# Bias tables of eight heads by one product and one spreading transfer, in a hybrid mLSTM, sparse-attention and mixture-of-experts layer

## The chip, the cores and the metric

The kernel runs on one core of a Trainium2 chip. The metric is the device time of one execution in microseconds (us), lower is better. The core has five engines that run their own instruction streams and meet at semaphores: TensorE (PE, matrix products), VectorE (DVE), ScalarE (ACT), GpSimd (POOL) and SyncE (SP, which here only issues transfers). ACT also issues transfers, from its own queue.

## The reference

One layer over 528 tokens (16 meta tokens and 512 real ones) of width 1024. After a layer norm, one wide projection feeds two branches: an mLSTM branch, and an attention branch that picks the 128 best keys of each query by an index score. Their outputs are gated, projected and normed, and a mixture of 16 experts follows. The part that matters here is the bias that the attention adds to its logits, a table lookup by bucket of the distance between query and key:

```python
def _rel_bucket(dist):
    n = jnp.maximum(dist, 0)
    nf = jnp.maximum(n, REL_MAX_EXACT).astype(jnp.float32)
    large = REL_MAX_EXACT + (jnp.log(nf / REL_MAX_EXACT) / math.log(REL_MAX_DIST / REL_MAX_EXACT)
                             * (REL_BUCKETS - REL_MAX_EXACT)).astype(jnp.int32)
    large = jnp.minimum(large, REL_BUCKETS - 1)
    return jnp.where(n < REL_MAX_EXACT, n, large)

        l_sel = jnp.einsum('bqhr,bqkr->bqhk', ql, c_sel) + \
            rel_bias[_rel_bucket(t[None, :, None] - sel)].transpose(0, 1, 3, 2)
        l_sel = jnp.where(valid[:, :, None, :], l_sel.astype(jnp.float32), -jnp.inf)
        p = jax.nn.softmax(jnp.concatenate([l_meta.astype(jnp.float32), l_sel], axis=-1), axis=-1)
```

`rel_bias` has 32 buckets by 8 heads. The bias depends only on the distance, so for one head it is one row of 656 numbers, and each query reads that row with its own shift.

## The kernel before

Every engine's program is one straight list in the code, and that order is the order of its work. Nothing is moved by a scheduler.

**The tables.** A one-hot matrix `oneh` (32 buckets by 656 distances) and `rel_bias` in `relb` (32 by 8) are loaded first. For each head h, `tables` on PE (L1057 to L1064) takes column h of `relb`, repeated 128 times, as the 32 by 128 weights and `oneh` as the moving operand, in two matmuls of 512 and 144 columns. That gives the head's row 128 times over, one copy in each of the 128 partitions of the accumulator `wide[h % 2]`. ACT copies it to one of four buffers in `ftab` (`tables_out`, L662) and issues a transfer of 328 KB to `table_dram[h]` (`tables_store`, L668). Eight such transfers write 8 x 128 equal rows to memory. Much later SP loads `strips` (L429) with a stride of 655 elements between rows of 656, which shifts each partition by one place: that is the bias of each query.

**Where they stand on PE.** Two heads at a time, between the projections:

- `tables(0)` at the very start, before the transposes of the input (L1075);
- `tables(2)` after the first unit's product, whose accumulators end with `kv_done`, and before `by_channel` of block `B_QI`;
- `tables(4)` after block `B_QI + 1`, and behind it the four small transposes L1126, which wait for `c_ready`;
- `tables(6)` after those transposes and before `channel_unit(2, B_QA)`.

**The projections around them.** The weights of the input projection come in units of 1 MB. SP loads a unit into `raw` (L394), ACT makes the high part `w_hi` (`split_hi`, L654), DVE the low part `w_lo` (`split_lo`, L1481), and PE multiplies three times (L1027, L1028, L1029: high by high, and the two mixed products). One 128 by 512 block is 24 such matmuls.

**The step that `c_ready` stands for.** PE transposes the compressed keys (L1116 to L1121, `ckv_done`), ACT squares them (L716), ACT does `split_hi(2)`, DVE does `split_lo(2)`, and DVE writes `c_tok` (L1530, `c_ready`). Before the squares ACT has three small functions on `rows` (L706 to L708), which in the kernel before stand behind `tables_out(2)`. DVE then goes on with scans on `rows` (L1535 to L1542), `widx`, which needs L1126, and `split_lo(3)`. The rounds of top-k on DVE start when ACT has put out the first index scores (L748), which PE makes in `index_scores(0)` (L1111) after `channel_unit(2, B_QA)`.

**Memory on the chip.** `ftab` lies where `v_ext` lies later. For that reason POOL waits at L550 for all eight stores before it writes the ones of `v_ext` (L552).

Of the kernel before, what the change touches and what calls it, by code (L numbers as in the profile page):

```python
# [8 lines left out]
F32 = mybir.dt.float32  # L9
# [6 lines left out]
ACT = mybir.ActivationFunctionType  # L16
# [3 lines left out]
P = 128  # L20
# [9 lines left out]
AH, AD = 8, 64  # L30
# [3 lines left out]
BUCKETS, MAX_EXACT, MAX_DIST = 32, 16, 128  # L34
# [22 lines left out]
FX = STRIP + P - 1 + 1  # L57
# [27 lines left out]
def build(nc, a, onehot, router_const, entries, no_token, slot_numbers, out, h_dram, table_dram, h1_dram, list_dram, y_dram):  # L85
    w_in = a["w_in"][0].rearrange("(c p) n -> p c n", p=P)
    with ExitStack() as ctx:
        base = 16640

        def at(name, shape, dtype, kb):  # L90
            return nc.alloc_sbuf_tensor_at(name, shape, dtype, offset=base + int(kb * 1024))

        def sem(name):
            return ctx.enter_context(nc.semaphore(name))
# [7 lines left out]
        def little(name, shape, dtype=F32):  # L102
# [40 lines left out]
        relb = little("relb", [BUCKETS, AH])  # L143
# [18 lines left out]
        A0 = 62.0  # L162
# [43 lines left out]
        ftab = at("ftab", [P, 4, FX], F32, A0 + 51)  # L206
        oneh = at("oneh", [BUCKETS, FX], F32, A0 + 139.5)
# [47 lines left out]
        wide = [ctx.enter_context(nc.psum_tensor(f"wide{i}", [P, 1024], F32)) for i in range(2)]  # L255
# [9 lines left out]
            table_in wuk_loaded table_done table_out strips_loaded  # L265
# [14 lines left out]
            late_consts z_added var1_ready rstd1_ready h1t_done h1t_used h1t_out h1_ready h1_stored gained  # L280
# [6 lines left out]
        q = {n: sem(n) for n in names}  # L287
        x_loaded = [sem(f"x_loaded{i}") for i in range(TT + 1)]
        table_stored = [sem(f"table_stored{i}") for i in range(2)]
# [91 lines left out]
        def _(sp):  # L381
# [42 lines left out]
            for stored in table_stored:  # L424
                sp.wait_ge(stored, 16 * AH // 2)
# [70 lines left out]
        def _(pool):  # L496
# [53 lines left out]
            for stored in table_stored:  # L550
                pool.wait_ge(stored, 16 * AH // 2)
# [95 lines left out]
        def _(act):  # L647
# [8 lines left out]
            def tables_out(h0):  # L656

                for h in (h0, h0 + 1):
                    act.wait_ge(q["table_done"], h + 1)
                    if h >= 4:  # L660
                        act.wait_ge(table_stored[h % 2], 16 * (h // 2))
                    nc.scalar.activation(ftab[:, h % 4, :], wide[h % 2][:, 0:FX], ACT.Copy).then_inc(q["table_out"], 1)  # L662

            def tables_store(h0):

                for h in (h0, h0 + 1):
                    act.wait_ge(q["table_out"], h + 1)
                    act.dma_start(table_dram[h], ftab[:, h % 4, :]).then_inc(table_stored[h % 2], 16)  # L668

            tables_out(0)  # L670

            for i in range(TT):
# [20 lines left out]
            tables_store(0)  # L693
# [9 lines left out]
            tables_out(2)  # L703
            tables_store(2)
# [308 lines left out]
        def _(pe):  # L1013
# [43 lines left out]
            def tables(h0):  # L1057

                for h in (h0, h0 + 1):
                    if h >= 2:  # L1060
                        pe.wait_ge(q["table_out"], h - 1)
                    rb = relb[:, h:h + 1].to_broadcast([BUCKETS, P])
                    nc.tensor.matmul(wide[h % 2][:, 0:512], rb, oneh[:, 0:512], start=True, stop=True)
                    nc.tensor.matmul(wide[h % 2][:, 512:FX], rb, oneh[:, 512:FX], start=True, stop=True).then_inc(q["table_done"], 1)  # L1064


            pe.wait_ge(q["table_in"], 32)
            tables(0)

            pe.wait_ge(q["table_out"], 2)  # L1070
# [44 lines left out]
            tables(2)  # L1115
# [7 lines left out]
            tables(4)  # L1123
# [4 lines left out]
            tables(6)  # L1128
            channel_unit(2, B_QA)
            pe.wait_ge(q["table_out"], AH)  # L1130
# [56 lines left out]
            for h in range(MH + 1):  # L1187
# [808 lines left out]
```

## Time and profile before

| | us |
|---|---|
| median of 3 runs | 871.2 |
| the runs | 869.11, 871.20, 873.55 |
| the profiled execution, device time | 869.1 |
| its span in the trace | 867.0 |
| PE busy | 761.4 (88% of the span) |
| DVE busy | 588.9 (68%) |
| ACT busy | 429.5 (50%) |
| POOL busy | 103.2 (12%) |

The span is the time from the first to the last record of the trace, and 2.1 us of the device time lie around it. "Idle before" is the time that an engine did nothing before an instruction, with the instruction or transfer that released it. The chain of waits is read backwards from the last instruction and shows only what the end waited for. PEclk is the clock that TensorE was granted: 1.00 is 2.4 GHz, 0.50 is 1.2 GHz, and a number between the two is a stretch that had both.

### The profile page before, as it was taken

The page shows a single profiled execution, that of the slowest core. Times are in us where ns is not written, and L with a number is a line of the kernel's source. Part 1 is how long each engine was busy: PE and PEld are TensorE (multiplying, and loading weights), DVE is VectorE, ACT ScalarE, POOL GpSimd, SP SyncE. Part 2 cuts the span into 40 slices and gives each one's busy share as a digit, 9 for nine tenths or more (in the row PEclk, how much of TensorE's full clock was granted, in tenths as well). Part 3 has the DMA queues.
Part 4 walks back from the last instruction along what each step waited for, and adds up shares of the span by engine and source line. Part 5 has one row for each costly group of instructions (what it writes and reads, how often), then busy time and mean ns, then how long its engine had stood idle before and what let it go on. Part 6 is the DMA issues. An engine that isn't in the chain of part 4 may idle for free.

```text
span 867.0 us, 10824 instructions
## 1 busy us (share of the span) xinstructions
PE 761.4 (88%) x3991; PEld 612.9 (71%) x3991; DVE 588.9 (68%) x794; ACT 429.5 (50%) x497; POOL 103.2 (12%) x118
## 2 busy tenths in 40 slices
PE   4499999999898787999999874899999999999920
PEld 2387799897566446887888773788888888888720
DVE  4905899795346644222464868788989888889838
ACT  5344433434542655322122130678787787787713
POOL 4630000000001000000000111212121111112012
PEclk9999999999999898999999975999999999999975
DMA  7744121310070300135126974699999999996143
GB/s 192 228 153 160 49 87 61 98 49 1 0 246 1 98 1 1 49 98 194 50 96 221 408 262 137 224 334 409 403 395 393 400 398 394 392 388 264 62 174 138
DMA packets 102644, 167.07 MB, mean 193 GB/s; under 512 B 18960, under 2 KB 39696, under 8 KB 102608
## 3 DMA queue, kind: packets, MB, share of 16 engines
q1 hardware_dynamic: 95024, 145.53, 47.4%
q0 software_dynamic: 4752, 13.11, 3.9%
q10 hardware_dynamic: 2832, 7.93, 2.3%
q8 instruction: 24, 0.39, 0.2%
q14 instruction: 12, 0.10, 0.0%
HBM read 153.38 MB, written 17.40 MB: 197 GB/s over the span
## 4 chain that ended last, share of the span: by engine, by line
PE 79%; DVE 8%; ACT 5%; issue 3%; DMA 2%; SPq 1%; POOL 0%; POOLq 0%; DVEq 0%; ACTq 0%
PE low L1027 15%; PE low L1028 15%; PE low L1029 15%; PE wide L1027 7%; PE wide L1029 7%; PE wide L1028 7%; PE wide L1390 2%; ACT prob L860 2%; PE low L1211 1%; PE low L1274 1%; PE low L1342 1%; PE wide L1196 1%; SPq L394 1%; PE low L1208 1%; PE low L1397 1%
## 5 line engine op out<-in xcount | busy, mean ns | idle before, releaser
L1760 DVE TENSOR_TENSOR m_lo<-m_raw,m_hi 128x2048 fp32r<-128x2048 f32 x95 | 215.0, 2290 | 30.2 <-ACT m_hi L906 29.6
L906 ACT ACTIVATE m_hi<-m_raw 128x2048 fp32r<-128x2048 f32 x95 | 179.7, 1917 | 27.8 <-PE low L1029 27.8
L1481 DVE TENSOR_TENSOR w_lo<-raw,w_hi 128x2048 fp32r<-128x2048 f32 x28 | 64.1, 2290 | 81.0 <-ACT w_hi L654 80.6
L1027 PE MATMUL low<-m_hi,xe_hi 128*128 128x512 f32 x256 | 104.4, 408 | 3.6 <-DVE xe_lo L1825 3.2
L1027 PE MATMUL low<-hT_hi,w_hi 128*128 128x512 f32 (+1 forms) x240 | 94.0, 392 | 10.6 <-issue 10.6
L1028 PE MATMUL low<-m_lo,xe_hi 128*128 128x512 f32 x256 | 101.5, 397 | 0.0
L1029 PE MATMUL low<-m_hi,xe_lo 128*128 128x512 f32 x256 | 101.4, 396 | 0.0
L1028 PE MATMUL low<-hT_lo,w_hi 128*128 128x512 f32 (+1 forms) x240 | 93.3, 389 | 0.0
L1029 PE MATMUL low<-hT_hi,w_lo 128*128 128x512 f32 (+1 forms) x240 | 92.6, 386 | 0.0
L654 ACT ACTIVATE w_hi<-raw 128x2048 fp32r<-128x2048 f32 x28 | 53.5, 1909 | 17.8 <-PE wide L1029 8.3
L1027 PEld LDWEIGHTS low<-hT_hi,w_hi 128*128 128x128 f32 x240 | 46.9, 195 | 20.9 <-issue 11.1
L1027 PEld LDWEIGHTS low<-m_hi,xe_hi 128*128 128x128 f32 x256 | 49.0, 191 | 17.2 <-DVE m_lo L1760 4.0
L1029 PEld LDWEIGHTS low<-m_hi,xe_lo 128*128 128x128 f32 x256 | 49.0, 192 | 10.9
L1028 PEld LDWEIGHTS low<-m_lo,xe_hi 128*128 128x128 f32 x256 | 49.0, 192 | 9.3
L1029 PEld LDWEIGHTS low<-hT_hi,w_lo 128*128 128x128 f32 x240 | 46.9, 195 | 9.1
L1028 PEld LDWEIGHTS low<-hT_lo,w_hi 128*128 128x128 f32 x240 | 46.8, 195 | 9.1 <-issue 0.2
L1027 PE MATMUL wide<-m_hi,hd_hi 128*128 128x512 f32 x128 | 51.3, 401 | 1.6 <-DVE hd_lo L1834 1.6
L1029 PE MATMUL wide<-m_hi,hd_lo 128*128 128x512 f32 x128 | 50.1, 391 | 0.0
L1028 PE MATMUL wide<-m_lo,hd_hi 128*128 128x512 f32 x128 | 49.8, 389 | 0.0
L730 ACT ACTIVATE gate<-low 128x512 f32<-128x512 f32 x16 | 9.6, 598 | 61.8 <-PE low L1029 61.8
L938 ACT ACTIVATE xe_hi<-wide 128x1024 fp32r<-128x1024 f32 x16 | 16.4, 1026 | 43.8 <-PE wide L1390 43.8
L1027 PE MATMUL wide<-hT_hi,w_hi 128*128 128x264 f32 x128 | 36.9, 288 | 1.1 <-ACT relu L748 1.0
(341 smaller groups left out, 1479.5 us busy)
## 6 DMA issues: line engine op xcount, KB each, us to landing
m_raw<-in_w_gate SPq DMA_DIRECT2D x32, 1024.0 KB, 9.4
m_raw<-in_w_up SPq DMA_DIRECT2D x32, 1024.0 KB, 8.7
m_raw<-in_w_down SPq DMA_DIRECT2D x31, 1024.0 KB, 10.4
raw<-in_w_in SPq DMA_DIRECT2D x19, 1024.0 KB, 5.5
raw<-in_w_out SPq DMA_DIRECT2D x4, 1024.0 KB, 4.9
table_dram<-ftab ACTq DMA_DIRECT2D x8, 328.0 KB, 3.2
strips<-table_dram SPq DMA_DIRECT2D x8, 264.0 KB, 4.2
xn<-in_x SPq DMA_DIRECT2D x4, 512.0 KB, 5.6
```

The costliest lines, as they stand in the source:

```text
L394: sp.dma_start(unit3(raw, u % RAW, u)[:, :, to:to + n], src).then_inc(raw_loaded[u % RAW], 16)
L654: nc.scalar.activation(w_hi[:, u % SPL, :], raw[:, u % RAW, :], ACT.Copy).then_inc(q["hi_ready"], 1)
L730: nc.scalar.activation(dst, src, func).then_inc(q["block_out"], 1)
L860: nc.scalar.activation(prob[:, h, 0:w], prob[:, h, 0:w], ACT.Exp, scale=-1.0, bias=nmax[:, h:h + 1], accum_out=psums[:, h:h + 1]).then_inc ...
L906: nc.scalar.activation(m_hi[n % MS][:, :], (m_spare if is_last(n, j) else m_raw[slot])[:, :], ACT.Copy).then_inc(q["m_hi_ready"], 1)
L938: nc.scalar.activation(xe_hi[:, :, :], wide[1][:, :].rearrange("p (c x) -> p c x", c=KC), ACT.Copy).then_inc(q["xe_hi_ready"], 1)
L1027: nc.tensor.matmul(outp, lh, rh, start=first, stop=False)
L1028: nc.tensor.matmul(outp, lh, rl, start=False, stop=False)
L1029: return nc.tensor.matmul(outp, ll, rh, start=False, stop=last)
L1390: mm = nc.tensor.transpose(wide[1][:, c * P:(c + 1) * P], xg[slot][:, c * P:(c + 1) * P], ident[:, :])
L1481: v.tensor_tensor(w_lo[:, u % SPL, :], raw[:, u % RAW, :], w_hi[:, u % SPL, :].bitcast(F32), ALU.subtract).then_inc(q["lo_ready"], 1)
L1760: v.tensor_tensor(m_lo[n % MS][:, :], (m_spare if is_last(n, j) else m_raw[n % MR])[:, :], m_hi[n % MS][:, :].bitcast(F32), ALU.subtract). ...
```

## The change

PE makes one pair of matmuls with the whole of `relb` (32 by 8) as weights: 8 output rows, one for each head. ACT copies them once to `ftab`, now 8 partitions by 656 at another address, and stores them to a new tensor in memory, `table_row`, 8 by 656. After `split_hi(3)`, ACT waits for that store and issues one transfer from memory to memory whose source names each row 128 times. It writes the same `table_dram` as before. The other three `tables` calls on PE, the copies and stores that went with them on ACT, and the waits on them are gone, on POOL too.

```diff
-        ftab = at("ftab", [P, 4, FX], F32, A0 + 51)
+        ftab = at("ftab", [AH, FX], F32, A0 + 128)
...
             sp.wait_ge(q["st_done"], MH)
-            for stored in table_stored:
-                sp.wait_ge(stored, 16 * AH // 2)
+            sp.wait_ge(q["table_stored"], 16)
...
             step(nc.gpsimd.memset(pre[:, :, 0:CONV - 1], 0.0))
-            for stored in table_stored:
-                pool.wait_ge(stored, 16 * AH // 2)
...
-            tables_out(0)
+            act.wait_ge(q["table_done"], 1)
+            nc.scalar.activation(ftab[:, :], wide[0][0:AH, 0:FX], ACT.Copy).then_inc(q["table_out"], 1)
+            act.wait_ge(q["table_out"], 1)
+            act.dma_start(table_row, ftab[:, :]).then_inc(q["table_put"], 16)
...
             split_hi(1)
-            tables_store(0)
...
             act.wait_ge(q["load_late"], 16 * 10)
-            tables_out(2)
-            tables_store(2)
...
             evac(B_QI, qidxT[:, 0, :])
-            tables_out(4)
-            tables_store(4)
             evac(B_QI + 1, qidxT[:, 1, :])
             split_hi(3)
-            tables_out(6)
-            tables_store(6)
+            act.wait_ge(q["table_put"], 16)
+            act.dma_start(table_dram, table_row.rearrange("h (o f) -> h o f", o=1).to_broadcast([AH, P, FX])).then_inc(q["table_stored"], 16)
...
             pe.wait_ge(q["table_in"], 32)
-            tables(0)
-
-            pe.wait_ge(q["table_out"], 2)
+            nc.tensor.matmul(wide[0][0:AH, 0:512], relb[:, :], oneh[:, 0:512], start=True, stop=True)
+            nc.tensor.matmul(wide[0][0:AH, 512:FX], relb[:, :], oneh[:, 512:FX], start=True, stop=True).then_inc(q["table_done"], 1)
+            pe.wait_ge(q["table_out"], 1)
...
-            tables(2)
             by_channel(take(B_QI)[:, :], 1, 0, META, T).then_inc(q["block_done"], 1)
...
             by_channel(take(B_QI + 1)[:, :], 1, P, META, T).then_inc(q["block_done"], 1)
-            tables(4)
             pe.wait_ge(q["c_ready"], TT + 1)
...
             mm.then_inc(q["wt_done"], 1)
-            tables(6)
             channel_unit(2, B_QA)
-            pe.wait_ge(q["table_out"], AH)
             pe.wait_ge(q["block_out"], B_QI + 2)
```

Line numbers of the changed kernel differ from here on: L1007, L1008 and L1009 are the products L1027, L1028 and L1029, and L1094 is the transpose L1126.

On PE, the place between block `B_QI + 1` (its last matmuls stand first) and `channel_unit(2, B_QA)`, before the change:

```order
171 L1028 MATMUL low<-hT_lo,w_hi 128x512
172 L1029 MATMUL low<-hT_hi,w_lo 128x512
173 L1063 MATMUL wide<-oneh,relb 128x512 [waits table_out]
174 L1064 MATMUL wide<-oneh,relb 128x144
175 L1063 MATMUL wide<-oneh,relb 128x512 [waits table_out]
176 L1064 MATMUL wide<-oneh,relb 128x144
177 L1126 MATMUL low<-ident,smallT 128x8 [waits c_ready]
178 L1126 MATMUL low<-ident,smallT 128x8 x3
179 L1063 MATMUL wide<-oneh,relb 128x512 [waits table_out]
180 L1064 MATMUL wide<-oneh,relb 128x144
181 L1063 MATMUL wide<-oneh,relb 128x512 [waits table_out]
182 L1064 MATMUL wide<-oneh,relb 128x144
```

The same place on PE after the change:

```order
165 L1008 MATMUL low<-hT_lo,w_hi 128x512
166 L1009 MATMUL low<-hT_hi,w_lo 128x512
167 L1094 MATMUL low<-ident,smallT 128x8 [waits c_ready]
168 L1094 MATMUL low<-ident,smallT 128x8 x3
169 L1007 MATMUL low<-hT_hi,w_hi 128x512 [waits lo_ready,hi_ready,block_out]
```

The transposes that wait for `c_ready` now follow the block directly, and the next projection follows them.

On ACT, the place from `split_hi(2)` (a `w_hi` row) to the copies of `qaT`, before the change:

```order
34 L654 ACTIVATE w_hi<-raw 128x2048 [waits kv_done,raw_loaded2]
35 L730 ACTIVATE qidxT<-low 128x512 [waits block_done,h_stored]
36 L662 ACTIVATE ftab<-wide 128x656 [waits table_stored0,table_done]
37 L662 ACTIVATE ftab<-wide 128x656 [waits table_stored1,table_done]
38 L668 DMA table_dram<-ftab 128x656 [waits table_out] x2
39 L730 ACTIVATE qidxT<-low 128x512 [waits block_done]
40 L654 ACTIVATE w_hi<-raw 128x2048 [waits block_done,raw_loaded0]
41 L662 ACTIVATE ftab<-wide 128x656 [waits table_stored0,table_done]
42 L662 ACTIVATE ftab<-wide 128x656 [waits table_stored1,table_done]
43 L668 DMA table_dram<-ftab 128x656 [waits table_out] x2
44 L730 ACTIVATE qaT<-low 128x512 [waits block_done] x2
```

The same place on ACT after the change:

```order
31 L650 ACTIVATE w_hi<-raw 128x2048 [waits kv_done,raw_loaded2]
32 L712 ACTIVATE qidxT<-low 128x512 [waits block_done,h_stored]
33 L712 ACTIVATE qidxT<-low 128x512 [waits block_done]
34 L650 ACTIVATE w_hi<-raw 128x2048 [waits block_done,raw_loaded0]
35 L719 DMA table_dram<-table_row 1024x1x656 [waits table_put]
36 L712 ACTIVATE qaT<-low 128x512 [waits block_done] x2
```

Four copies and four stores have left this stretch, and one transfer with its wait has come behind `split_hi(3)`.

## Rows read from the trace of the kernel before

**Rows 1.** The page, the chain of waits by engine, shares of the span.

```profile
PE 79%; DVE 8%; ACT 5%; issue 3%; DMA 2%; SPq 1%; POOL 0%; POOLq 0%; DVEq 0%; ACTq 0%
```

**Rows 2.** The chain of waits in order of time: start, length, engine, tile, line.

```profile
54.47 1.05 PE wide L1063 x2
...
56.87 0.43 PE low L1027
57.30 0.23 PE low L1028
...
68.77 1.05 PE wide L1063 x2
...
71.19 0.84 PE wide L1063 x2
...
73.38 0.72 PE low L1027
74.10 0.43 PE low L1028
...
76.97 0.23 PE low L1029
```

**Rows 3.** Timeline of PE from 68 us: start, length, engine, line, tiles.

```profile
70.78 0.29 PE L1126 MATMUL low<-ident,smallT 8*128 8x8 f32 x2
...
71.01 1.02 PE L1063 MATMUL wide<-oneh,relb 32*128 32x512 f32 x2
```

**Rows 4.** Timelines of ACT and DVE from 36 us, idle time in brackets.

```profile
58.03 0.73 ACT L706 ACTIVATE rows<-smallT,bif 4x528 f32<-4x528 f32 x1 [0.41 <-ACT ftab L662]
...
63.23 0.28 ACT L716 ACTIVATE md<-low 128x128 f32<-128x128 f32 x1 [1.84 <-PE low L1120]
...
67.15 2.29 DVE L1481 TENSOR_TENSOR w_lo<-raw,w_hi 128x2048 fp32r<-128x2048 f32 x1 [1.46 <-ACT w_hi L654]
69.36 1.37 DVE L1530 SCALAR_TENSOR_TENSOR c_tok<-low,crs,kvg 128x128 f32<-128x128 f32 x5
...
76.79 2.29 DVE L1481 TENSOR_TENSOR w_lo<-raw,w_hi 128x2048 fp32r<-128x2048 f32 x1
87.80 0.35 DVE L1556 TENSOR_SCALAR score<-relu,widx 128x256 f32<-128x256 f32 x1 [8.71 <-ACT relu L748]
```

**Rows 5.** Stretches: busy time and count of each engine, PEclk, DMA share, GB/s.

```profile
69.80:73.20 3.40, 3.40 (x19) 1.90 (x17) 3.30 (x7) 2.31 (x4) 0.00 (x0) 1.00 0.79 234
73.20:76.60 3.40, 3.40 (x10) 2.62 (x9) 3.23 (x6) 2.20 (x2) 0.00 (x0) 0.52 0.77 275
```

**Rows 6.** PE's timeline at three later gaps, and the stretches of 3 us behind them.

```profile
219.18 1.16 PE L1192 MATMUL low<-rows,sel_row 4*128 4x512 f32 x2 [2.55 <-DVE dw L1646]
...
219.00:222.00 3.00, 2.83 (x4) 0.42 (x4) 0.72 (x2) 1.80 (x3) 0.00 (x0) 0.68 0.00 0
...
317.02 0.40 PE L1247 MATMUL wide<-khT,qaT 64*128 64x16 f32 x4 [2.28 <-DVE nmax L1683]
...
318.00:321.00 3.00, 2.66 (x20) 1.71 (x20) 1.68 (x5) 1.41 (x4) 0.00 (x0) 1.00 0.00 0
...
327.85 0.40 PE L1247 MATMUL wide<-khT,qaT 64*128 64x16 f32 x4 [2.66 <-DVE nmax L1683]
...
330.00:333.00 3.00, 3.00 (x17) 2.57 (x15) 1.34 (x5) 1.39 (x3) 0.00 (x0) 0.55 0.00 0
```

**Rows 7.** Transfers: table stores, the strips' issues, SP's loads of units.

```profile
table_dram<-ftab ACTq DMA_DIRECT2D x8, 328.0 KB, 3.2
...
L429 SPq DMA_DIRECT2D strips<-table_dram x8: 339/432/547, 243.3 to 246.5; - x8
...
69.47 31.16 SPq L394 DMA_DIRECT2D raw<-in_w_in  x3
```

**Rows 8.** Timeline of ACT in the first 10 us.

```profile
8.12 0.72 ACT L662 ACTIVATE ftab<-wide 128x656 f32<-128x656 f32 x1 [1.47 <-PE wide L1064]
...
9.23 1.24 ACT L674 ACTIVATE xn<-xn,shift,rstd 128x1024 f32<-128x1024 f32 x1 [0.39 <-DVE shift L1488]
```

More of the change, by code:

```diff
@@ L82, in bcast_rows, with build @@
     return bass.AP(tensor=ap.tensor, offset=ap.offset + offset, ap=[[0, P], [1, n]])
-def build(nc, a, onehot, router_const, entries, no_token, slot_numbers, out, h_dram, table_dram, h1_dram, list_dram, y_dram):
+def build(nc, a, onehot, router_const, entries, no_token, slot_numbers, out, h_dram, table_row, table_dram, h1_dram, list_dram, y_dram):
     w_in = a["w_in"][0].rearrange("(c p) n -> p c n", p=P)
@@ L264, in build @@
             const_done vec_step act_step pool_step zero_done
-            table_in wuk_loaded table_done table_out strips_loaded
+            table_in wuk_loaded table_done table_out table_put table_stored strips_loaded
             load_consts load_late
@@ L279, in build @@
             z_part h_loaded  vm_ready
-            late_consts z_added var1_ready rstd1_ready h1t_done h1t_used h1t_out h1_ready h1_stored gained
+            late_consts z_added var1_ready rstd1_ready h1t_done h1t_used h1t_out h1_ready h1_stored
             router_done scores_ready chosen_ready  dest_ready  listed lists_loaded lists_ready
@@ L288, in build @@
         x_loaded = [sem(f"x_loaded{i}") for i in range(TT + 1)]
-        table_stored = [sem(f"table_stored{i}") for i in range(2)]
         gathered = [sem(f"gathered{i}") for i in range(2)]
@@ L654, in split_hi @@
                 nc.scalar.activation(w_hi[:, u % SPL, :], raw[:, u % RAW, :], ACT.Copy).then_inc(q["hi_ready"], 1)
[L656 to L668, printed above, removed]
-            tables_out(0)
+            act.wait_ge(q["table_done"], 1)
+            nc.scalar.activation(ftab[:, :], wide[0][0:AH, 0:FX], ACT.Copy).then_inc(q["table_out"], 1)
+            act.wait_ge(q["table_out"], 1)
+            act.dma_start(table_row, ftab[:, :]).then_inc(q["table_put"], 16)
             for i in range(TT):
@@ L1055, in by_token @@
                 return mm
[L1057 to L1064, printed above, removed]
             pe.wait_ge(q["table_in"], 32)
-            tables(0)
-            pe.wait_ge(q["table_out"], 2)
+            nc.tensor.matmul(wide[0][0:AH, 0:512], relb[:, :], oneh[:, 0:512], start=True, stop=True)
+            nc.tensor.matmul(wide[0][0:AH, 512:FX], relb[:, :], oneh[:, 512:FX], start=True, stop=True).then_inc(q["table_done"], 1)
+            pe.wait_ge(q["table_out"], 1)
             pe.wait_ge(q["const_done"], 1)
@@ L1982 @@
     h_dram = nc.dram_tensor("h_dram", (S, D), F32, kind="Internal").ap()
+    table_row = nc.dram_tensor("table_row", (AH, FX), F32, kind="Internal").ap()
     table_dram = nc.dram_tensor("table_dram", (AH, P, FX), F32, kind="Internal").ap()
@@ L1993 @@
     y_dram = nc.dram_tensor("y_dram", (2 * S, D), F32, kind="Internal").ap()
-    build(nc, a, oh, router_const, entries, no_token, slot_numbers, out, h_dram, table_dram, h1_dram, list_dram, y_dram)
+    build(nc, a, oh, router_const, entries, no_token, slot_numbers, out, h_dram, table_row, table_dram, h1_dram, list_dram, y_dram)
     return run(nc, [arrays], core_ids=[0]).results[0]["out"]
```

## The prediction

> **What bounds the kernel now.** I read the chain of waits first, because the change takes work off PE and that is worth something only where PE is what the end waits for. 79% of the span hangs on PE [rows 1]. In the order of time the chain runs through the three later table calls. From 54.47 to 56.87 us it is the tables of heads 2 and 3, from 68.77 to about 70.8 those of heads 4 and 5, from 71.19 to 73.38 those of heads 6 and 7, each with PE products right before and right behind [rows 2]. The first table call, at 3 to 8 us, is not in the chain at all. Next I read the timelines of PE, DVE and ACT around 70 us, to see what would be late once the tables are gone [rows 3, 4]. Then I read the granted clock there and behind other gaps of PE [rows 5, 6], and last the transfers [rows 7].
>
> **The start.** Two heads' tables, two copies and two buffers become one pair of matmuls, one copy and one small store. ACT's second copy ran from 8.12 to 8.84 us, and ACT then stood idle 0.39 us until DVE's shift released it for the first tile of the input at 9.23 [rows 8]. So DVE was the later one there, and the copy that goes gives back nothing. The new store is issued by ACT behind the first copy, about 6.7 us. A table store costs ACT's queue some 0.4 us, which fits before 9.23. Worth: 0.
>
> **Tables of heads 2 and 3.** They hold PE, in the chain, from 54.47 to 56.87: 2.40 us [rows 2]. The block behind them needs nothing of ACT that is late: it uses unit 1, split long before. It starts 2.40 us earlier, and so do the transposes of the compressed keys behind it. Worth: 2.40.
>
> **Tables of heads 4 and 5.** Here the gain goes. Before the change PE ends these tables at about 70.8 and starts the small transposes L1126 at 70.78 [rows 3]. Those wait for `c_ready`, and DVE ended `c_tok` at 69.36 + 1.37 = 70.73 [rows 4]. Table work and wait end together, so the tables were filling a wait of PE. How far does `c_ready` move? Follow it back. DVE's `c_tok` stands right behind `split_lo(2)` at 67.15, which ACT's `w_hi` released. That follows ACT's squares, the first of which, at 63.23, had been idle 1.84 us for PE's transposes [rows 4]. So the whole row of steps hangs on PE and moves by the same 2.40 us. ACT's three functions on `rows` ran before the squares and started at 58.03, behind a table copy [rows 4]. They move at least as far, since the copies ahead of them go. So `c_ready` comes at 70.73 - 2.40 = 68.33. Block `B_QI + 1` ends at 68.77 - 2.40 = 66.37 [rows 2]. PE now stands idle from 66.4 to about 68.4, where it computed tables before. The call was 2.0 us long and the new wait is 2.0 us long. Worth: 0.
>
> **Tables of heads 6 and 7.** They stand behind the transposes, from 71.19 to 73.38 in the chain: 2.19 us [rows 2]. `channel_unit(2)` needs the split of unit 2, which DVE ends before `c_tok`. Worth: 2.19. Its start moves from 73.38 to 68.79, that is 2.40 + 2.19 = 4.59 us. The PE timeline gives nearly the same (the transposes start at 70.78 and the tables 0.23 later [rows 3], so 4.6 to 4.7).
>
> **Does it pass through?** DVE ends the scans and starts `split_lo(3)` at 76.79, and then idles 8.71 us until ACT's first index scores, at 87.80 [rows 4]. Those come from PE, behind `channel_unit(2)`. DVE's own work ahead of the idle moves by 2.4 us and has 8.71 us of slack, less the 2.2 us by which PE moves further. So DVE, too, starts its top-k rounds 4.6 us earlier. ACT loses four copies of 0.72 us there, as the one shown [rows 8], and gets one issue. POOL's write to `v_ext` moves earlier and nobody waits for it yet. SP's unit loads wait for DVE's `lo_ready`, and move with it. Every later stage starts on one of these.
>
> **The clock.** Through the stretch in which PE ran tables of 32 rows, 69.8 to 73.2, the granted clock was 1.00, and in the next, 73.2 to 76.6, it was 0.52 [rows 5], so nearly all at 1.2 GHz. The 8 matmuls from 73.38 to 76.97 took 3.59 us [rows 2]. At the 0.23 us of the full clock they take 1.87, plus 0.20 for the first of a block (0.43 at 56.87 against 0.23 behind it). So the fall cost 1.5 us. After the change PE idles 2.0 us and then does only tiny transposes for 0.2 to 0.4. Does the clock fall again? Three gaps of PE in this trace are near. Behind 2.55 us of idle the next 3 us had 0.68, behind 2.66 us the stretch from 330 us had 0.55, and behind 2.28 us the clock stayed at 1.00 [rows 6]. With its transposes the new gap is 2.2 to 2.4 us, just among them. At one end the fall stays as it was (worth 0), at the other it goes (worth 1.5). I take 0, since two of three near gaps fell, but it is close to even, and the next run may differ from the last one.
>
> **The transfer.** It writes the same 2.6 MB as the eight stores did. The stores landed after 3.2 us each [rows 7], so 8 in a row take at most 25.6 us. The new one also reads memory, so up to twice that by this estimate, 51 us. It starts behind `split_hi(3)`, at about 69 us (the block before it ends at 66.4, and two short ACT instructions and the split of 1.9 follow), and SP's first load of strips is issued at 243.3 [rows 7], 4.6 us earlier after the change: about 170 us of cover. It shares the engines with the loads of units 6 and 7, issued in the stretch from 69.47 to 100.6 [rows 7]. These are 1 MB each and are split on ACT some 30 us or more behind their issue, so a few us more are hidden. Worth: 0. If the cover were gone it would cost its length beyond 170 us.
> The rows show nothing of how a repeated source is spread over the 16 DMA engines. The Trainium skill, "DMA: Bandwidth & Descriptors", section "Rules for kernel authors", says that the slowest dimension of the access patterns sets the number of engines, so that an outermost dimension under 16 confines a transfer to at most so many. The source here has 8 rows outermost, which would mean 8 engines, a doubling of the 51 us to about 100, an estimate. It would still be under the cover. No row of before shows it.
>
> **Sum.** 0 + 2.40 + 0 + 2.19 + 0 = 4.6 us. The profiled execution took 869.1 (867.0 of span and 2.1 around it), so it becomes 864.5. The median of the runs stands 2.1 above it. From the median, 871.2 - 4.6 = 866.6.
>
> **Rivals.**
> (a) The clock holds. Then 1.5 us more are gained: 6.1, which gives 865.1. For it: the gap at 317 us, and that the tables of 4.6 us in a row, the longer stretch of poor work, are gone. Against it: the other two gaps.
> (b) The clock pays more than before. The fall comes with a second one, since every later gap of PE meets the clock at another moment. One fall costs 1.5, as worked out above: 4.6 - 1.5 = 3.1, which gives 868.1.
> (c) The gain is hidden anyway. If `c_ready` or the first index scores depended on something that doesn't move (a load, a store), PE would wait there up to the old time: gain 0 to 2.4, 871.2 to 868.8. Against it: each step above was released by PE or its followers [rows 4].
> (d) Slower: the transfer is confined to very few DMA engines. If the eight stores at 3.2 us were spread over all 16 and this one is on one, it takes 8 x 3.2 x 16 = 410 us, from 69 to 479, and SP's wait for it ends 240 us late: about 1107. It decides from 170 us on, that is 6.6 times the 25.6. Below that it costs nothing. For it, only the odd shape of the source. Against it: 128 rows for each head.
>
> **How the numbers follow.** Forecast 0.45, (a) 0.30, (b) 0.14, (c) 0.08, (d) 0.03. The range takes in the forecast, (a) and most of (b), and for its ends the medians' own scatter, since three runs of before spread over 4.4 us: 863.2 to 869.8. About 0.5%, 4.4 us, is what a measurement of this kernel can tell from no change, so the line is at 866.8, right beside the forecast. Of the forecast a bit over half falls under it (0.27), of (a) nearly all (0.28), of the rest 0.02: faster 0.57. Slower, (d) and a bad draw of the clock: 0.05. The rest, 0.38, is the same.
>
> **What would show each step.** PE has two table matmuls, at about 3 us, and none later. Block `B_QI` starts at about 54.4. The four transposes wait for DVE's `c_tok` with about 2.0 us idle of PE before them, and start at 68.4. `channel_unit(2)` starts at 68.8. The first score on DVE comes at about 83.2, with idle time before it as now. The clock behind 68.8 tells forecast from (a): 0.5 or 1.00 for some 3 us. The spreading transfer lands before 170 us. The prediction is wrong if PE's wait for `c_ready` is longer than 2.3 us, if the strips' issues move by other than 4 to 6 us, or if the distance between them and the end of the span changes by over 2 us.

## The result, and the profile after

| | before | after |
|---|---|---|
| median, us | 869.45 (6 runs) | 863.5 (6 runs) |
| lowest to highest | 866.82 to 873.55 | 860.06 to 865.65 |
| profiled execution, device time | 869.1 | 863.86 |
| its span | 867.0 | 861.9 |
| PE busy | 761.4 | 751.6 |

The ratio of after to before is 0.9925, 95% interval 0.9903 to 0.9948: 6.5 us less, 4.5 to 8.4 (the two medians differ by 6.0). The kernel is faster by more than the 0.5% that this measurement can tell. The forecast had been 4.6 us, so the way was right and the size, by the best estimate, too small; 4.6 lies just inside the interval. The absolute time, 863.5, lies at the very edge of the range of 863.2 to 869.8. Measured once more beside other kernels, the change came to 0.9939 (0.9919 to 0.9959), 5.3 us.

On the page of after, the end still hangs on PE, as in [rows 1]:

```profile
PE 751.6 (87%) x3961; PEld 605.7 (70%) x3963; DVE 588.9 (68%) x794; ACT 424.6 (49%) x490; POOL 103.5 (12%) x118
...
PE 78%; DVE 8%; ACT 6%; issue 4%; DMA 2%; SPq 1%; POOL 1%; POOLq 0%; DVEq 0%; ACTq 0%
```

The timeline of PE after the change, in place of the tables of [rows 2, 3] (start, length, engine, line, tiles, idle time before in brackets):

```profile
65.00 0.39 PE L1009 MATMUL low<-hT_hi,w_lo 128*128 128x512 f32 x1
67.40 0.41 PE L1094 MATMUL low<-ident,smallT 8*128 8x8 f32 x4 [2.02 <-DVE c_tok L1496]
67.74 0.50 PE L1007 MATMUL low<-hT_hi,w_hi 128*128 128x512 f32 x1
...
69.57 0.63 PE L1007 MATMUL low<-hT_hi,w_hi 128*128 128x512 f32 x1
...
72.43 0.40 PE L1008 MATMUL low<-hT_lo,w_hi 128*128 128x512 f32 x1
```

The block ends at 65.2, PE stands idle for 2.02 us, released by DVE's `c_tok`, and the next projection starts at 67.74, where it was at 73.3. The first four matmuls behind it still start 0.23 to 0.34 us apart; from 68.8 to about 72.2 they start 0.43 apart.

ACT and DVE around it, answering [rows 4]:

```profile
59.84 0.28 ACT L698 ACTIVATE md<-low 128x128 f32<-128x128 f32 x1 [2.05 <-PE low L1089]
...
63.77 2.29 DVE L1447 TENSOR_TENSOR w_lo<-raw,w_hi 128x2048 fp32r<-128x2048 f32 x1 [1.46 <-ACT w_hi L650]
65.98 1.36 DVE L1496 SCALAR_TENSOR_TENSOR c_tok<-low,crs,kvg 128x128 f32<-128x128 f32 x5
...
82.25 0.35 DVE L1522 TENSOR_SCALAR score<-relu,widx 128x256 f32<-128x256 f32 x1 [6.54 <-ACT relu L728]
```

The row of steps is the same as before: the squares wait for PE's transposes, the low part of the split for ACT's high part, `c_tok` for the split. The first score on DVE comes 5.55 us earlier than in [rows 4], and DVE still idles ahead of it.

The stretches of 3 us with the granted clock (third number from the right), answering [rows 5]:

```profile
66.00:69.00 3.00, 1.60 (x9) 1.40 (x10) 2.90 (x9) 1.82 (x2) 0.00 (x0) 0.97 0.49 138
69.00:72.00 3.00, 3.00 (x8) 2.32 (x8) 2.91 (x3) 0.00 (x0) 0.00 (x0) 0.50 0.95 314
72.00:75.00 3.00, 3.00 (x14) 2.36 (x13) 2.89 (x4) 0.00 (x0) 0.00 (x0) 0.96 0.52 197
```

The clock fell to 1.2 GHz at about 68.8, 1.1 us into the projection behind the gap. Before the change it fell behind the tables.

ACT's rows at the same place show when the spreading transfer was issued:

```profile
65.52 0.77 ACTq L719 DMA_DIRECT2D table_dram<-table_row  x1
65.92 1.90 ACT L650 ACTIVATE w_hi<-raw 128x2048 fp32r<-128x2048 f32 x1
```

In the code the transfer stands behind `split_hi(3)`, the second row. In the trace it was issued at 65.52, before that split began at 65.92.

The start, answering [rows 8], and the issues of the strips, answering [rows 7]:

```profile
8.71 1.24 ACT L659 ACTIVATE xn<-xn,shift,rstd 128x1024 f32<-128x1024 f32 x1 [2.10 <-DVE shift L1454]
...
L427 SPq DMA_DIRECT2D strips<-table_dram x8: 339/432/609, 237.8 to 241.1; - x8
```

ACT now idles 2.10 us ahead of the first tile, again released by DVE. The strips start at 237.8, 5.5 us earlier than before, and the span is 5.1 us shorter. Not all of the 5.5 is the change: the last product of the first unit, which stands ahead of the tables of heads 2 and 3, already came 0.8 us earlier in this profile (53.42 against 54.19, shown below).

### The profile page after: what moved, and what is told of

Its sections match the earlier page's. It is cut to its first block, busy times and chain, and to the rows that moved or that the text cites. A ratio compares the mean times of both kernels' runs of the same rounds, so it can differ in the third digit from the quotient of the medians.

```text
span 861.9 us, 10746 instructions
## 1 busy us (share of the span) xinstructions
PE 751.6 (87%) x3961; PEld 605.7 (70%) x3963; DVE 588.9 (68%) x794; ACT 424.6 (49%) x490; POOL 103.5 (12%) x118
## 4 chain that ended last, share of the span: by engine, by line
PE 78%; DVE 8%; ACT 6%; issue 4%; DMA 2%; SPq 1%; POOL 1%; POOLq 0%; DVEq 0%; ACTq 0%
PE low L1007 15%; PE low L1009 15%; PE low L1008 15%; PE wide L1007 7%; PE wide L1009 7%; PE wide L1008 7%; PE wide L1356 2%; ACT prob L840 2%; PE low L1177 1%; ACT w_hi L650 1%; PE wide L1162 1%; PE low L1308 1%; PE low L1240 1%; SPq L393 1%; PE low L1174 1%
## 5 line engine op out<-in xcount | busy, mean ns | idle before, releaser
L1007 PE MATMUL low<-m_hi,xe_hi 128*128 128x512 f32 x256 | 103.9, 406 | 3.6 <-DVE xe_lo L1791 3.2
L1007 PE MATMUL low<-hT_hi,w_hi 128*128 128x512 f32 (+1 forms) x240 | 93.6, 390 | 10.6 <-issue 10.6
L1009 PE MATMUL low<-m_hi,xe_lo 128*128 128x512 f32 x256 | 100.8, 394 | 0.0
L1008 PE MATMUL low<-m_lo,xe_hi 128*128 128x512 f32 x256 | 100.4, 392 | 0.0
L1008 PE MATMUL low<-hT_lo,w_hi 128*128 128x512 f32 (+1 forms) x240 | 93.2, 388 | 0.0
L1009 PE MATMUL low<-hT_hi,w_lo 128*128 128x512 f32 (+1 forms) x240 | 92.7, 386 | 0.0
L1007 PEld LDWEIGHTS low<-hT_hi,w_hi 128*128 128x128 f32 x240 | 46.8, 195 | 20.6 <-issue 11.0
L1007 PEld LDWEIGHTS low<-m_hi,xe_hi 128*128 128x128 f32 x256 | 48.6, 190 | 17.2 <-DVE m_lo L1726 4.4
L1009 PEld LDWEIGHTS low<-m_hi,xe_lo 128*128 128x128 f32 x256 | 48.5, 189 | 10.9
L1008 PEld LDWEIGHTS low<-m_lo,xe_hi 128*128 128x128 f32 x256 | 48.7, 190 | 9.2
L1008 PEld LDWEIGHTS low<-hT_lo,w_hi 128*128 128x128 f32 x240 | 46.6, 194 | 9.2 <-issue 0.2
L1009 PEld LDWEIGHTS low<-hT_hi,w_lo 128*128 128x128 f32 x240 | 46.7, 194 | 9.0
L1007 PE MATMUL wide<-m_hi,hd_hi 128*128 128x512 f32 x128 | 51.3, 401 | 1.6 <-DVE hd_lo L1800 1.6
L1009 PE MATMUL wide<-m_hi,hd_lo 128*128 128x512 f32 x128 | 50.1, 392 | 0.0
L1008 PE MATMUL wide<-m_lo,hd_hi 128*128 128x512 f32 x128 | 49.8, 389 | 0.0
L1007 PE MATMUL wide<-hT_hi,w_hi 128*128 128x264 f32 x128 | 36.9, 288 | 1.1 <-ACT relu L728 1.0
```

What stands on the lines that cost most here:

```text
L1007: nc.tensor.matmul(outp, lh, rh, start=first, stop=False)
L1008: nc.tensor.matmul(outp, lh, rl, start=False, stop=False)
L1009: return nc.tensor.matmul(outp, ll, rh, start=False, stop=last)
```

## A measure that doesn't depend on the start

Two profiles of one kernel can differ by a few us, so a comparison of two spans is weak. The first dense product (L1027 of before) started at 39.85, 39.77 and 38.42 us in three profiles of the same kernel before, and the three spans were 867.0, 871.3 and 867.3. I therefore use stretches between two events in one profile: **A**, from PE's transposes of the compressed keys (L1120, L1089 after) to DVE's first score (L1556, L1522), and **B**, from that first score to the first issue of the strips. All 14 profiles, in us:

| kernel | A | B |
|---|---|---|
| before, first profile | 25.2 | 155.5 |
| before, second | 26.8 | 155.6 |
| before, third | 25.2 | 157.2 |
| before, split first | 26.8 | 155.5 |
| no first pair | 26.9 | 155.5 |
| no second pair | 26.8 | 155.5 |
| no third pair | 26.7 | 155.5 |
| no fourth pair | 21.4 | 157.2 |
| change, first profile | 23.0 | 155.6 |
| change, second | 23.0 | 155.6 |
| change, POOL waits | 23.0 | 155.5 |
| change, gap filled | 21.4 | 155.6 |
| change, split first | 19.4 | 155.6 |
| change, split first, other spreading | 19.4 | 155.6 |

B is 155.5 or 155.6 in all but two, so nothing between the first score and the strips depends on the tables. A takes few values, and they are what the experiments below explain.

The tables of heads 2 and 3 stand ahead of A and are not in it. What they held is read between the last product of the first unit and the transposes. Before:

```profile
54.19 0.28 PE L1029 MATMUL low<-hT_hi,w_lo 128*128 128x264 f32 x1
54.40 1.12 PE L1063 MATMUL wide<-oneh,relb 32*128 32x512 f32 x2
...
56.80 0.50 PE L1027 MATMUL low<-hT_hi,w_hi 128*128 128x512 f32 x1
57.14 0.40 PE L1028 MATMUL low<-hT_lo,w_hi 128*128 128x512 f32 x1
...
62.59 0.60 PE L1120 MATMUL low<-ident,cT 128*128 128x128 f32 x4
...
73.31 0.79 PE L1027 MATMUL low<-hT_hi,w_hi 128*128 128x512 f32 x1
```

After:

```profile
53.42 0.28 PE L1009 MATMUL low<-hT_hi,w_lo 128*128 128x264 f32 x1
53.54 0.40 PE L1007 MATMUL low<-hT_hi,w_hi 128*128 128x512 f32 x1
...
59.21 0.60 PE L1089 MATMUL low<-ident,cT 128*128 128x128 f32 x4
```

From the start of the first row to the transposes it is 62.59 - 54.19 = 8.40 us before and 59.21 - 53.42 = 5.79 after. The seven profiles with those tables have 8.40 or 8.41, the seven without them 5.78 or 5.79: the call held PE for 2.6 us.

The stretch behind B, from the first issue of the strips to the end, is where single profiles scatter: 621.8 to 628.3 us over the 14. The six profiles of before in which the tables of heads 4 to 7 are all left have a mean of 625.0 there, and the six of the change and its variants 625.0 as well. So nothing of the gain is seen there, and much of the scatter of the times is.

## The experiments

### One pair of tables at a time

Each of the first four takes one `tables` pair out of the kernel before, with its copies and stores. For the first pair:

```diff
-            tables_out(0)
...
-            tables_store(0)
...
-            tables(0)
-
-            pe.wait_ge(q["table_out"], 2)
```

and the counts of the semaphores go down by two heads. The others are the same for `tables(2)`, `tables(4)` and `tables(6)`.

> The kernel before without the table matmuls, copies and stores of heads 0 and 1 at the start (those two heads' bias is left out; their strips are loaded from heads 2 and 3). Theory of the prediction: DVE releases the first tile of the input, so the start gives nothing: same as before, and the first dense product starts at about 39.8 us as before. Rival: the start is the source of the surplus of the change, 0.7 to 1.5 us faster, and the first dense product starts at about 39.1 us.

Ratio 1.0008 (0.9986 to 1.0031): no difference, 869.0 against 869.4. The interval reaches down to 1.2 us less, so the times alone don't exclude the lower part of the rival's 0.7 to 1.5. The first dense product starts at 39.51, but three profiles of before spread from 38.42 to 39.85, so that number decides nothing. The row of ACT for the first tile of the input decides:

```profile
9.27 1.24 ACT L675 ACTIVATE xn<-xn,shift,rstd 128x1024 f32<-128x1024 f32 x1 [7.18 <-DVE shift L1487]
```

With no table work ahead of it ACT stood idle for 7.18 us and still began at 9.27, where it began at 9.23 in [rows 8]: DVE sets this time, and the start gives nothing.

> The kernel before without the tables of heads 2 and 3 (left out; their strips come from heads 4 and 5). Theory: PE gets back 2.40 us in full, since everything behind follows PE, and the wait for c_ready moves with it: 2.4 us faster. Rival: something that doesn't move holds c_ready or the scores, and the gain is under 1 us.

Ratio 0.9978 (0.9956 to 1.0001), 1.9 us less with an interval from 0 to 3.8. It holds the 2.4 and leans against the rival's "under 1", but doesn't exclude it. The profile is clearer: the next block follows the first unit's product directly, and from that product to the transposes it is 5.79 us in place of 8.40, so 2.6 less. A behind it, 26.8, is a value that before has too. So nothing that doesn't move took the gain back.

> The kernel before without the tables of heads 4 and 5 (left out; their strips come from heads 6 and 7). Theory: they filled PE's wait for c_ready, so PE stands idle 2.0 us in their place and the gain is 0 to 0.2 us. Rival: the copies on ACT that go with them also delayed c_ready or later work, and the gain is 1 to 2 us.

Ratio 0.9996 (0.9977 to 1.0016), 0.3 us: nothing, as the theory had it, though the interval reaches to 2.0 less and so doesn't exclude the rival. The timeline of PE in this kernel does:

```profile
68.68 0.22 PE L1126 MATMUL low<-ident,smallT 8*128 8x8 f32 x1 [2.02 <-DVE c_tok L1530]
```

The wait of 2.02 us stands where the tables were. From the transposes of the compressed keys to these small ones it is 8.20 us, and 8.19 in before and after: the copies that went too did not bring `c_ready` forward. Removing the call gave nothing because it had filled a wait of the same length.

> The kernel before without the tables of heads 6 and 7 (left out; their strips come from heads 0 and 1). Theory: PE gets back 2.19 us. If the clock fell because of 4.6 us of table work in a row, it now sees only 2.1 us of it and may hold: then 3.7 us. Rival: the clock falls as before in most runs and the gain stays at 2.2.

Ratio 0.9966 (0.9949 to 0.9983), 3.0 us less (1.5 to 4.4), between the two, and both are inside the interval. In its profile the clock held where the kernel before fell to 0.72 and 0.50:

```profile
69.00:72.00 3.00, 3.00 (x19) 2.50 (x18) 2.90 (x4) 2.21 (x3) 0.00 (x0) 1.00 0.99 301
72.00:75.00 3.00, 3.00 (x15) 2.44 (x14) 2.83 (x6) 0.91 (x1) 0.00 (x0) 1.00 0.71 262
```

A is 21.4, against 25.2: 3.8 less, that is 2.19 of tables and 1.6 of clock. B, though, is 157.2 here, 1.7 longer: behind the gap of PE that ends at 213.6 us the clock stayed down for longer than it did behind the same gap in the first profile of before. So of the 3.8 only 2.1 are left by the time the strips are issued (A + B is 178.6 against 180.7; against the later profiles of before, with 182.3 and 182.4, it is 3.7). With 2.1 us of table work in a row the clock held at the tables in this one profile, and with 4.6 us it fell in every one.

### The change again, and the clock behind the gap

> The changed kernel itself, timed once more, beside the next three. Theory of the prediction: the steps give 4.6 us, so the ratio to the kernel before is 0.9947, and the larger gain first measured was scatter of the draws. Rival: there is something more in the change, and the ratio stays at 0.9925 (6.5 us).

Ratio 0.9939 (0.9919 to 0.9959), 5.3 us, between the theory's 4.6 and the rival's 6.5, and both are inside the interval. Timing alone can't tell them apart. The profile shows A at 23.0 once more.

The next one fills the gap of PE with work of its own:

```diff
+            for i in range(8):
+                nc.tensor.matmul(bank[4][:, :], hT_hi[:, i, 0:P], hT_hi[:, i, META:T], start=(i == 0), stop=(i == 7))
             pe.wait_ge(q["c_ready"], TT + 1)
```

> The changed kernel with 8 dense matmuls of 128 x 512 (1.9 us, result unused) put into PE's 2.0 us of idle before the transposes that wait for c_ready. Theory: the fall of the clock behind the gap comes from PE standing idle; with dense work in it the clock holds and the kernel is 1.5 us faster than the change. Rival: the fall has to do with something else (its place in time), it stays, and the time is that of the change.

Ratio to before 0.9928 (0.991 to 0.9945), median 863.1 against 864.1 of the change in the same series. The intervals of the two ratios overlap for the most part, so the times don't settle it. The profile does: PE's filler (first row) is followed by stretches at the full clock.

```profile
63.96 2.02 PE L1093 MATMUL wide<-hT_hi 128*128 128x512 f32 x8
...
66.00:69.00 3.00, 2.88 (x15) 2.42 (x16) 2.86 (x5) 0.56 (x1) 0.00 (x0) 1.00 0.85 276
69.00:72.00 3.00, 3.00 (x15) 2.43 (x14) 2.87 (x5) 0.00 (x0) 0.00 (x0) 1.00 0.70 243
```

A falls from 23.0 to 21.4. The transposes still wait until `c_ready`, so the 1.6 us are the clock alone. In all three profiles of the change with the gap open the clock fell, and in the one with dense work in it, it held. The fall comes from the idle gap, and costs 1.6. The next experiment, which closes the gap in another way, is the second case in which it held.

### The order of the split

The edit moves one split, on both engines:

```diff
@@ ACT
+            split_hi(2)
             act.wait_ge(q["ckv_done"], 1)
...
             square.then_inc(q["css_ready"], 1)
-            split_hi(2)
@@ DVE
             split_lo(1)
+            split_lo(2)
...
             v.tensor_scalar(css[0:META, TT:TT + 1], ...).then_inc(q["cvar_ready"], 1)
-            split_lo(2)
```

> The changed kernel with the split of unit 2 (high part on ACT, low part on DVE) put ahead of the squares, into ACT's 2.05 us and DVE's idle time before them. Theory: c_ready comes 2 us or more earlier, PE's gap of 2.0 us goes, and with it the fall of the clock: 2.0 + 1.5 = 3.5 us faster than the change. Rival: the wait moves to another place (the squares start late because the split of 1.9 us is in front of them, or PE waits for the split of unit 3) and the gain is under 1 us.

Ratio to before 0.989 (0.9872 to 0.9908), median 860.2, 3.9 us under the change in the same series. The timeline of PE shows no wait:

```profile
65.66 0.39 PE L1009 MATMUL low<-hT_hi,w_lo 128*128 128x512 f32 x1
65.97 0.41 PE L1094 MATMUL low<-ident,smallT 8*128 8x8 f32 x4
66.32 0.50 PE L1007 MATMUL low<-hT_hi,w_hi 128*128 128x512 f32 x1
```

A is 19.4: 2.0 less than with the gap filled (the wait itself), and 3.6 less than the change (wait and clock). The expectation of 3.5 is met.

> The kernel before with only the split of unit 2 put ahead of the squares. Theory: in the kernel before PE doesn't wait for c_ready, since the tables of heads 4 and 5 fill that time, so the earlier c_ready gives nothing: same as before, within 0.5 us. The 3.5 us of the same edit on top of the change are then there only because the tables are gone. Rival: the edit is worth something by itself, 2 us or more.

Ratio 1.0003 (0.998 to 1.0025). The same edit on the kernel before gives nothing. There PE is still at the tables of heads 4 and 5 when `c_ready` comes: the small transposes run 7.3 us behind those of the keys in place of 8.2, in the middle of the table products, and A stays 26.8. Taking the tables out is what makes the split's place matter.

### The spreading transfer

The trace has no landing for the transfer itself, so the first of these makes it visible:

```diff
             step(nc.gpsimd.memset(pre[:, :, 0:CONV - 1], 0.0))
+            pool.wait_ge(q["table_stored"], 16)
```

> The changed kernel with POOL's wait for the spreading transfer put back before it writes the ones of v_ext, so that the write marks the landing. By the stores of before: 25.6 to 51 us after the issue at 65.5, so at 91 to 117 us. By the share of the transfer engines in the trace of the change (0.52 from 72 to 86 us): it runs on half of the 16 engines and lands at about 87. Nobody needs v_ext before about 102, so up to there the time is that of the change.

POOL's row for the write behind that wait:

```profile
84.41 0.13 POOL L549 MEMSET v_ext<- 128x20 f32 x1 [22.83 <-DMA table_dram<-table_row]
```

It landed at 84.3 us, having been issued at 63.3. In this profile PE, ACT and DVE ran 2.2 to 2.3 us earlier than in the first profile of after, so the 84.3 stands for about 86.5 there, where the shares had said about 87. The ratio, 0.9935 (0.9912 to 0.9959), is the change's. Two rows of the change's own trace while the transfer runs alone, and one after its end (second number from the right: share of the 16 transfer engines):

```profile
73.00:74.00 1.00, 1.00 (x6) 0.81 (x5) 0.93 (x3) 0.00 (x0) 0.00 (x0) 1.00 0.52 193
...
85.00:86.00 1.00, 1.00 (x6) 0.80 (x5) 0.93 (x4) 0.00 (x0) 0.00 (x0) 1.00 0.52 193
...
87.00:88.00 1.00, 1.00 (x6) 0.82 (x5) 0.93 (x4) 0.40 (x1) 0.00 (x0) 1.00 0.00 0
```

From issue to landing it took 84.3 - 63.3 = 21.0 us, and while it ran alone the mean busy share of the 16 transfer engines was 0.52, at 193 GB/s. The Trainium skill, "DMA: Bandwidth & Descriptors", section "Rules for kernel authors", says that an outermost dimension under 16 confines a transfer to at most that many engines. The trace agrees: 8 of 16 would give 0.50, and the share was 0.52, though the views used here don't name the engines. Of the two lengths that I had estimated, 51 us on all engines and 100 on eight, neither is near: it took 21.

The last experiment turns the order of the dimensions round, so that the 128 copies stand outermost on both sides, on top of the earlier split. Against the change, only this line differs besides the split:

```diff
-            act.dma_start(table_dram, table_row.rearrange("h (o f) -> h o f", o=1).to_broadcast([AH, P, FX])).then_inc(q["table_stored"], 16)
+            act.dma_start(table_dram.rearrange("h p f -> p h f"), bass.AP(tensor=table_row.tensor, offset=table_row.offset, ap=[[0, P], [FX, AH], [1, FX]])).then_inc(q["table_stored"], 16)
```

> The changed kernel with the split of unit 2 ahead of the squares, and with the spreading transfer written so that the 128 copies are the slowest dimension and the 8 heads the inner one. Theory: the transfer uses all 16 engines, so the share of the transfer engines is near 1.0 while it runs alone and it is over in about half of the 20 us; nobody waits for it, so the time is that of the run with the split first, about 9.5 us under the kernel before. Rival: the share stays near 0.52.

The page's row of the transfer (KB, us from issue to landing) and the stretches of 2 us after it in this kernel, the transfer having been issued at 63.4:

```profile
table_dram<-table_row ACTq DMA_DIRECT2D x1, 2624.0 KB, 11.5
```

```profile
72.00:74.00 2.00, 2.00 (x10) 1.64 (x9) 0.00 (x0) 0.00 (x0) 0.00 (x0) 1.00 0.94 327
...
76.00:78.00 2.00, 2.00 (x10) 1.62 (x10) 1.42 (x4) 1.95 (x5) 0.00 (x0) 1.00 0.64 225
78.00:80.00 2.00, 2.00 (x10) 1.62 (x9) 1.86 (x6) 1.07 (x1) 0.00 (x0) 1.00 0.00 0
```

The transfer lands after 11.5 us in place of 21.0, at 74.9. While it was under way the share was 0.79 to 1.04, with loads of units beside it, no stretch stands at 0.52 any more, and by 78 us everything that was under way is over. A and B are 19.4 and 155.6, exactly as with the split alone: PE waited for none of it. The ratio to before is 0.9866 (0.9835 to 0.9897), 11.7 us less (9.0 to 14.4), where 9.5 had been expected; medians 857.8 and 870.35. The split alone had 0.989 (0.9872 to 0.9908) in another series, and the two intervals overlap, so the faster transfer isn't shown to bring time. With over 150 us of cover it shouldn't. This kernel has the lowest ratio of all, and its interval lies clear of that of the change (0.9919 to 0.9959), but not of that of the split alone.

### The kernel before, twice more

So far the change's gain had come out at 6.5 and 5.3 us by the times, while the sum said 4.6. The profile of before had A at 25.2, where those without the first, second or third pair had 26.7 to 26.9. The open question was whether 25.2 or 26.8 is the kernel before. Both of these are the unchanged kernel.

> The kernel before, profiled once more. Theory now: the fall of the clock in the 4.6 us of table work comes at a varying place. Where it starts inside them, the tables of heads 6 and 7 run at 1.2 GHz too and the fall lasts about 6.8 us, not 3.4, so that from the transposes of the compressed keys to the first issue of the strips it takes 182.4 us (as in the run without the first pair) and not 180.7 (as in the first profile of before); the changed kernel always took 178.3 to 178.6. Rival: the first profile is typical, and this one shows 180.7 again and a fall of 3.4 us.

Span 871.3 us, 4.3 above the first profile of the same kernel. The timeline of PE and two stretches with the granted clock:

```profile
71.34 1.57 PE L1063 MATMUL wide<-oneh,relb 32*128 32x512 f32 x2
...
73.31 0.80 PE L1027 MATMUL low<-hT_hi,w_hi 128*128 128x512 f32 x1
...
77.32 0.63 PE L1027 MATMUL low<-hT_hi,w_hi 128*128 128x512 f32 x1
```

```profile
72.00:75.00 3.00, 3.00 (x8) 1.91 (x7) 2.90 (x4) 1.95 (x2) 0.00 (x0) 0.50 1.00 356
75.00:78.00 3.00, 3.00 (x8) 2.32 (x8) 2.90 (x4) 1.43 (x2) 0.00 (x0) 0.50 0.35 136
```

The two table products of 512 columns took 1.57 us in place of 1.02: here the clock fell while PE was still at the tables of heads 6 and 7, and it stayed down from 71.7 to 78.5, 6.8 us, where in the first profile it was down from 73.3 to 76.7. A is 26.8. The expectation of 182.4 is met: A + B is 182.3.

> The same again, for a third draw of the kernel before: 182.4 us and a fall of about 6.8 us by the theory that the place varies, 180.7 and 3.4 by the rival. A mix over the three draws also speaks for the theory.

Span 867.3. A is 25.2 and B 157.2. The sum of the two, 182.4, is what the theory had, but for another reason, and that is luck and no support for it. The short fall at the tables is back, 3.4 us long, and the missing 1.7 us were lost later, inside B, at the clock's next fall:

```profile
219.00:222.00 3.00, 3.00 (x4) 0.84 (x3) 0.60 (x1) 2.24 (x5) 0.00 (x0) 0.50 0.00 0
222.00:225.00 3.00, 3.00 (x7) 1.65 (x5) 0.00 (x0) 1.47 (x4) 0.00 (x0) 0.53 0.00 0
```

The same stretches had 0.68 and 0.75 in the first profile. So the kernel before has a short and a long fall, and the state of the clock is not the same from run to run. The kernel without the fourth pair had its 157.2 in B from the same place in the program. The theory that a fall which begins inside the table work is the long one does not hold as it was put. In this third profile the last two table products of 144 columns already ran slow, and the fall was short:

```profile
70.15 0.40 PE L1064 MATMUL wide<-oneh,relb 32*128 32x144 f32 x2
70.40 1.07 PE L1063 MATMUL wide<-oneh,relb 32*128 32x512 f32 x2
71.27 0.68 PE L1064 MATMUL wide<-oneh,relb 32*128 32x144 f32 x2
71.88 0.79 PE L1027 MATMUL low<-hT_hi,w_hi 128*128 128x512 f32 x1
```

### What A is made of

With the clock at 2.4 GHz throughout, A is 21.4 (gap filled, and no fourth pair). The tables of heads 6 and 7 behind the transposes add 2.2, which makes 23.6 for before. Its six profiles that still had both later table calls in a row give 25.2 twice and 26.8 four times: the fall costs 1.6 or 3.2, on average 2.7. The change gives 21.4 + 1.6 = 23.0 three times out of three. From 26.3, the mean of the six, to 23.0 are 3.3, and with the 2.6 of heads 2 and 3 the gain is 5.9 us, an estimate, since six and three profiles give the mix of falls only roughly. The one longer B among the six would add 0.3. The two measurements, 5.3 (3.6 to 7.0) and 6.5 (4.5 to 8.4), lie on both sides of it, and their intervals hold the forecast's 4.6 as well: it is the stretches of the traces, and not the times, that show the difference.

## Why the prediction was right or wrong

**The start, worth 0: right.** Removing the first pair alone gives 1.0008, and ACT waits for DVE's shift either way: 2.10 us after the change, 7.18 with no table work there at all.

**Heads 2 and 3, 2.40: right, and a little small.** PE gets the time back in full, and it is 2.6 us: 8.40 against 5.79 up to the transposes. The call itself is 56.80 - 54.40 = 2.40, but the changes to it and from it cost the other 0.2. The first table product starts 0.21 us behind the last product of the unit, where such products start 0.12 apart, and the first two products of the block start 0.34 apart, where it is 0.23 without the call. The time of the kernel without them, 1.9 us less, has both 2.4 and 2.6 inside its interval.

**Heads 4 and 5, 0: right.** The new wait was to be 2.0 us long and is 2.02, behind DVE's `c_tok`. Without those tables alone the kernel takes the same time, and with the split earlier the wait can be had back, but only once the tables are gone: 1.0003 on the kernel before.

**Heads 6 and 7, 2.19: right.** From the small transposes to the next projection it is 73.31 - 70.78 = 2.53 before and 67.74 - 67.40 = 0.34 after: 2.19.

**Pass-through: right.** B is 155.5 in before and 155.6 after, and DVE's first score still finds an idle engine. The strips' issues moved by 5.5, inside the 4 to 6 that I had named, of which 0.8 are a difference of the two starts. The first score came at 82.25 and not at 83.2: 0.8 of that is the start as well, and 0.2 are heads 2 and 3. From the strips' issue to the end it is 623.7 before and 624.1 after, inside the 2 us that I had allowed; but three profiles of before have 623.7, 627.2 and 624.1 there, so that sign could have failed by chance. Rival (c), that a part of the gain is hidden, is ruled out up to the strips.

**The transfer, 0: right.** It is over 150 us before the strips need it. I had it start at about 69, behind `split_hi(3)`; it was issued at 65.5, before that split. Rival (d), few engines, was right in its direction: the share was that of eight of sixteen, and not of the one engine that it priced, and 21 us is far from the 170 at which it would decide. My bounds of 51 and 100 us were both far too long.

**The clock, 0: this is the step that failed, a term of the sum that was mis-sized.** The step said that the fall after the change costs what the fall before cost, 1.5 us, read from one profile. The right half is that the clock fell behind the new gap, in all three profiles with that gap, and that this costs 1.6. That it fell I had called close to even, so this half is partly luck. The wrong half is the price before. I took it from the dense matmuls behind the tables in a profile that happened to hold the short fall. In four profiles out of six the fall costs 3.2: it begins on the table products, slows them too, and lasts 6.8 us in place of 3.4. The term is worth 0 or 1.6, and 1.1 on average. Rival (a), that the clock holds, gave a time, 865.1, that is nearer the measured one, but its mechanism did not happen. Rival (b), that the clock's falls cost more, had the sign the wrong way round.

**The starting point.** The forecast started at 871.2, the median of three runs. With more runs before came to 869.45 (6 runs), 869.4 (35), 869.7 (14) and 870.35 (17). So 1 to 2 us of the 3.1 between 866.6 and 863.5 come from that median, and the rest from the terms above (1.1 of the clock and 0.2 of heads 2 and 3) and from scatter. 869.45 - 5.9 = 863.55 comes out so near the measured 863.5 by luck: the six new runs alone spread over 5.6 us.

What stays open is why the fall is sometimes short and sometimes long. The start of the first dense product, 37.0 to 40.0 us over all profiles, doesn't sort them: 39.85 goes with 25.2 and 39.77 with 26.8. What does go with the length is how late the fall came. Counted from the first table product of heads 4 and 5, it came after 4.6 and 4.2 us in the two profiles with the short fall, and after 2.8 to 3.8 us in the four with the long one. No run set that moment, so this is a pattern of six profiles and not a cause.

## What to carry to other kernels

Work taken off the engine that bounds the kernel pays only where it doesn't fill a wait: ask for each piece what the next instruction there would wait for, and by when. Where such a wait appears, reorder what feeds it: one split moved on two engines gave 3.9 us more by the medians (3.6 in A), though the same move was worth nothing while the work was still there. Price a fall of the clock from several profiles of the same kernel, as one of them may hold the short one and the next the long one.

## What the runs showed of the hardware

- The granted clock fell to 1.2 GHz behind an idle gap of PE of 2.01 or 2.02 us in three profiles of three, and stayed at 2.4 GHz when the gap was filled with matmuls of 128 rows (one profile) or closed (two).
- It fell in all six profiles in which PE did fp32 products of 32 rows for two calls nearly in a row, 4.6 us, although PE was busy the whole time (3.00 of 3.00 us). With the last of the two calls removed it held, in the one profile taken. With the first of them removed, an idle gap of 2.02 us and then one call, it fell (A 26.7).
- The same kernel, run again, pays 1.6 or 3.2 us for the same fall: the clock was down for 3.4 or 6.8 us.
- A transfer from ACT's queue that had nothing left to wait for was issued at 65.52, ahead of the split of 1.9 us that stands before it in the code and began at 65.92.
- A transfer between two places in memory with 8 rows outermost ran at a mean busy share of 0.52 of the 16 transfer engines and took 21.0 us for 2624 KB. With the 128 copies outermost it took 11.5 us.
